# Five levels of a triangular inverse in one loop on quarters of the heads, with Y ahead of V behind it

## The chip, the cores and the metric

The kernel runs on one core of one Trainium2 chip. The metric is the device time of one execution, in microseconds; a kernel's time is the median over runs. A separate execution is profiled instruction by instruction, and its own time is given beside it.

## The reference

The program computes two transformer layers on one sequence of 256 tokens with 2048 features: a layer of two attention mixers, then a layer with an RWKV-7 recurrence beside a latent attention, and a gated feed-forward part. The change touches the recurrence alone. It has 16 heads of 64 features, and the reference runs it token by token:

```
def step(state, inp):
    r_t, w_t, k_t, v_t, a_t, b_t = inp
    sa = jnp.einsum('bhvk,bhk->bhv', state, a_t)
    state = (state * w_t[:, :, None, :]
             + sa[..., None] * b_t[:, :, None, :]
             + v_t[..., None] * k_t[:, :, None, :])
    return state, jnp.einsum('bhvk,bhk->bhv', state, r_t)
```

## The kernel before

Every engine has its own instruction stream, written out by hand, and semaphores join them. Most of the time goes to matrix products of a token block with weights that are split in a high and a low part (lines 973 to 1040 on TensorE, 1830 on ScalarE, 626 on GpSimd). Between the attention of the second layer and its output product stands the recurrence, called the scan here.

The scan cuts the 256 tokens into NCH = 4 chunks of 64. In a chunk it forms small 64x64 products for each of the 16 heads, inverts a unit lower triangular 64x64 matrix per head, and carries a 64x64 state to the next chunk. The heads stand in two sets `s` of 8: four pairs `q`, one head of a pair on partitions 0 to 63 and one on 64 to 127 (`halves`). A product for a set is 8 matmuls of 64x64, written by the generator `each`; each uses one quadrant of the array. With `swap=False` they use the two diagonal quadrants, with `swap=True` the other two; `in_turn` interleaves two generators, so that a swapped and an unswapped one run side by side. Every fp32 matmul shows as two records in the trace, so a product of a set is 16 records. Each set owns four PSUM banks (0 to 3).

The inverse is built by doubling in levels `m` = 1 to 5. In level m:

- GpSimd masks the matrix (`below_level`, M_m, line 900) into a buffer `LM`;
- TensorE makes T_m = M_m times X into bank 3 (`level_t`); VectorE adds the identity on its way out (`T2`, line 2695);
- TensorE makes X_m and Z_m from T_m side by side, into banks 0 and 1 (`level_xz`); ScalarE copies X_m out (line 2168), VectorE copies Z_m out (line 2705). In level 5 only Z_5, the inverse, is made.

The order on TensorE within chunk c: LB with P1 of chunk c-1; L; AK with U of chunk c-1; T1; S (the state's update) of chunk c-1; X1 and Z1; BK (transposed tokens, bank 2, copied by ScalarE at line 2189); then levels 2, 3 and 4 in an engine loop, `pe.Fori`, one pass a level, waits computed from the pass number (`wait_turn`); behind it, written out, level 5, Y of chunk c-1 (the outputs) and V, in this order: T5 in turn with the first half of Y, the second half of Y, V, Z5. After the last chunk P1, U and Y of chunk 3 follow. ScalarE copies P1, U, Y and V out (lines 2176 and 2168). ScalarE's last part has this order: P1 of chunk 3, four copies of the attention's output (line 2196), U, Y. TensorE then sums the outputs (line 1678) and starts the output product.

## Time and profile before

| | us |
|---|---|
| median of 3 runs | 1897.81 (1895.79 to 1908.44) |
| the profiled execution, its own time | 1894.01 |
| its span, first to last instruction | 1892.3 |
| the scan on TensorE, first LB to the sum behind the last Y | 943.58 to 1046.46 |

| engine | busy in the span | share |
|---|---|---|
| PE (TensorE) | 1832.4 us | 97% |
| POOL (GpSimd) | 1371.3 us | 72% |
| DVE (VectorE) | 1124.3 us | 59% |
| ACT (ScalarE) | 803.1 us | 42% |

Times in the views are microseconds from the span's start. PE rows are matmuls; a row's length counts the stay of the last matmul in the array. "issue" is time in which an engine waited for nothing that the profile shows. The chain of waits is followed back from the last instruction. The profiled execution is 3.8 us below the median.

### The profile page before, as it was taken

To read this page: it belongs to the slowest core of one execution; us is meant where nothing else is said; L and a number is where in the kernel's file an instruction comes from. 1 tells how busy PE (TensorE), PEld (TensorE's weight loads), DVE (VectorE), ACT (ScalarE), POOL (GpSimd) and SP (SyncE) were. 2 spreads that over 40 slices of the span, in tenths; PEclk is the share of its full clock that TensorE was granted. 3 is DMA by queue.
4 is the path that set the end of the run, shared out by engine and by line. 5 is a ranking of instruction groups with operands and counts; after the bars stand their busy time and mean duration, and the time that the engine had idled before them with its cause. 6 is when DMAs were issued, how large, how long until landed. Compare 5 with 4: busy or idle time off the path is not lost.

```text
span 1892.3 us, 31908 instructions
## 1 busy us (share of the span) xinstructions
PE 1832.4 (97%) x12663; PEld 1530.5 (81%) x12663; DVE 1124.3 (59%) x1207; ACT 803.1 (42%) x1079; POOL 1371.3 (72%) x693
## 2 busy tenths in 40 slices
PE   6999999999999999999898999999999999999998
PEld 3777778888668898888688788888888888788886
DVE  1225858560343546878664664788888888933235
ACT  4234444444454554343423554433333344343334
POOL 3657878888339889965353898999999989844443
PEclk9999999999999999999999999999999999999999
DMA  9996545555785565543200356655555555655552
GB/s 341 357 358 216 178 156 178 189 190 183 263 287 178 163 204 193 187 135 136 67 4 4 134 178 201 194 184 191 186 187 190 181 195 179 222 194 186 197 197 92
DMA packets 191066, 352.48 MB, mean 186 GB/s; under 512 B 6991, under 2 KB 52445, under 8 KB 188413
## 3 DMA queue, kind: packets, MB, share of 16 engines
q1 hardware_dynamic: 189580, 346.31, 55.5%
q10 hardware_dynamic: 1393, 4.83, 0.6%
q8 instruction: 70, 1.15, 0.2%
q14 instruction: 23, 0.19, 0.0%
HBM read 349.02 MB, written 2.10 MB: 186 GB/s over the span
## 4 chain that ended last, share of the span: by engine, by line
PE 66%; POOL 10%; issue 9%; DVE 9%; DMA 2%; SPq 2%; ACT 2%; POOLq 0%; DVEq 0%; ACTq 0%
POOL WL L626 10%; PE bank L1033 9%; PE bank L973 9%; PE bank L978 9%; PE bank L974 8%; PE bank L1040 5%; PE bank L1500 4%; PE bank L1784 4%; PE bank L1779 4%; PE bank L1777 4%; DMA arena<-in_w_ada 2%; SPq L689 2%; DVE arena L2437 2%; DVE CV L2778 1%; PE bank L419 1%
## 5 line engine op out<-in xcount | busy, mean ns | idle before, releaser
L626 POOL TENSOR_TENSOR WL<-WR,WH 128x1024 fp32r<-128x1024 f32 (+2 forms) x524 | 1269.0, 2447 | 379.9 <-ACT WH L1830 302.1
L1830 ACT ACTIVATE WH<-WR 128x1024 fp32r<-128x1024 f32 (+1 forms) x556 | 571.0, 1036 | 741.4 <-PE bank L1040 320.1
L1033 PE MATMUL bank<-HX,WH 128*128 128x512 f32 x1840 | 461.5, 392 | 0.0
L1033 PEld LDWEIGHTS bank<-HX,WH 128*128 128x128 f32 x1840 | 331.0, 189 | 59.0
L973 PE MATMUL bank<-WH,HX 128*128 128x512 f32 (+2 forms) x864 | 340.2, 394 | 2.7 <-ACT arena L1926 1.4
L974 PE MATMUL bank<-WH,HX 128*128 128x512 f32 (+2 forms) x864 | 331.0, 384 | 0.0
L1040 PEld LDWEIGHTS bank<-HX,WL 128*128 128x128 f32 x1840 | 250.4, 190 | 22.0 <-POOL WL L626 4.7
L1040 PE MATMUL bank<-HX,WL 128*128 128x256 f32 x1840 | 257.8, 283 | 1.1 <-POOL WL L626 0.6
L978 PE MATMUL bank<-WL,HX 128*128 128x512 f32 (+2 forms) x864 | 227.3, 385 | 1.9 <-POOL WL L626 1.4
L973 PEld LDWEIGHTS bank<-WH,HX 128*128 128x128 f32 x864 | 162.7, 188 | 43.7 <-issue 11.8
L978 PEld LDWEIGHTS bank<-WL,HX 128*128 128x128 f32 x864 | 159.3, 188 | 35.2 <-POOL WL L626 5.8
L974 PEld LDWEIGHTS bank<-WH,HX 128*128 128x128 f32 x864 | 162.8, 188 | 30.7 <-issue 2.2
L626 DVE TENSOR_TENSOR WL<-WR,WH 128x1024 fp32r<-128x1024 f32 x42 | 53.4, 1274 | 142.0 <-ACT WH L1830 142.0
L1777 PE MATMUL bank<-WH,AH 128*128 128x512 f32 x320 | 124.6, 389 | 0.0
L1779 PE MATMUL bank<-WH,AL 128*128 128x512 f32 x320 | 124.5, 389 | 0.0
L2778 DVE TENSOR_SCALAR CV<-RAWF,cols 128x256 f32<-128x256 f32 x44 | 102.0, 2378 | 2.0 <-DVE RAWF L2536 2.0
L2783 DVE SCALAR_TENSOR_TENSOR CV<-RAWF,cols,CV 128x256 f32<-128x256 f32 x44 | 100.0, 2331 | 1.6 <-DVE CV L2778 1.5
L2437 DVE TENSOR_SCALAR arena<-arena,small 128x128 f32<-128x128 f32 x64 | 69.6, 1156 | 31.1 <-ACT small L1838 31.1
L1784 PE MATMUL bank<-WL,AH 128*128 128x512 f32 x320 | 85.7, 390 | 2.0 <-DVE WL L626 2.0
L900 POOL TENSOR_TENSOR arena<-half,masks 128x256 f32<-128x256 f32 x40 | 29.0, 744 | 69.0 <-DVE half L2683 48.1
L1784 PEld LDWEIGHTS bank<-WL,AH 128*128 128x128 f32 x320 | 60.0, 188 | 14.7 <-DVE WL L626 2.4
L1777 PEld LDWEIGHTS bank<-WH,AH 128*128 128x128 f32 x320 | 60.1, 188 | 12.5
(347 smaller groups left out, 2088.0 us busy)
## 6 DMA issues: line engine op xcount, KB each, us to landing
WR<-in_w_in SPq DMA_DIRECT2D x80, 1024.0 KB, 5.0
WR<-in_ffn_w_gate SPq DMA_DIRECT2D x44, 1024.0 KB, 5.2
WR<-in_ffn_w_up SPq DMA_DIRECT2D x44, 1024.0 KB, 5.1
WR<-in_ffn_w_down SPq DMA_DIRECT2D x42, 1024.0 KB, 5.0
arena<-in_w_ada SPq DMA_DIRECT2D x64, 512.0 KB, 9.0
WR<-in_w_out SPq DMA_DIRECT2D x32, 1024.0 KB, 5.0
WR<-in_w_in SPq DMA_DIRECT2D x32, 512.0 KB, 8.9
WR<-in_w_ada SPq DMA_DIRECT2D x16, 1024.0 KB, 5.0
```

What stands on the lines that cost most here:

```text
L626: last = eng.tensor_tensor(lo[:, k, :], raw[:, k, :], hi[:, k, :], ALU.subtract)
L973: pe.matmul(out, hx[:, 0, kk, o], w, start=start, stop=False, skip_group_check=True)
L974: return pe.matmul(out, hx[:, 1, kk, o], w, start=False, stop=False, skip_group_check=True)
L978: return pe.matmul(out, hx[:, 0, kk, t * P:(t + 1) * P], w, start=False, stop=stop, skip_group_check=True)
L1033: last = pe.matmul(BANK[(first + f) % 8][:, :].rearrange("p (h n) -> p h n", h=2), wh[:, k, f * P:(f + 1) * P], hx[:, :, kk, :], start=kk ...
L1040: last = pe.matmul(BANK[(first + f) % 8][:, 0:L], wl[:, k, f * P:(f + 1) * P], hx[:, 0, kk, :], start=False, stop=kk == KT - 1, skip_group ...
L1777: pe.matmul(BANK[2 * c + t][:, :], AH[:, g % 2, k, o], wh[:, k, :], start=first and k == 0, stop=False, skip_group_check=True)
L1779: last = pe.matmul(BANK[2 * c + t][:, :], AL[:, g % 2, k, o], wh[:, k, :], start=False, stop=False, skip_group_check=True)
L1784: last = pe.matmul(BANK[2 * c + t][:, :], AH[:, g % 2, k, t * P:(t + 1) * P], wl[:, k, :], start=False, stop=final and k == PK - 1, skip_g ...
L1830: act.activation(half(WH, nth(n) % 2, *w), half(WR, n % NSLOT, *w), ACT.Copy).then_inc(hi_ready, 1)
L2437: last = dve.tensor_scalar(v, v, hr[:, g:g + 1], None, ALU.mult)
L2778: own.mark(dve.tensor_scalar(CV[:, f, :], RAWF[:, f, 2:L + 2], w(2), cols[:, ds(4 * i + (cb + f), 1)], ALU.mult, ALU.add))
```

## The change

The heads are treated in four quarters `g` (set `g // 2`, two of its four pairs) from level 2 on, and level 5 goes through the loop, which so makes four passes and not three.

- In a pass TensorE makes T for the four quarters, 4 matmuls each, then X and Z for the four, 8 matmuls each. Level 5 makes an X too, which nobody copies. Even quarters use bank 3 for T and Z and bank 0 for X, odd ones bank 1 for T and Z and bank 2 for X.
- VectorE copies T of all quarters and Z of quarters 0 and 1, ScalarE X of all quarters and Z of quarters 2 and 3, each copy 128x128 and not 128x256. T of a quarter now waits for the copy of its Z as well as of its X, since both use one bank.
- Bank 2 holds BK before the loop, so TensorE waits for both copies of BK ahead of it.
- The buffer for M5 is dropped: M2 to M5 share one, and each waits for T of the level before of both quarters of its set.
- Behind the loop stands Y of chunk c-1 alone, then V. Y and V wait for the copies of Z5; P1 of the next chunk still waits for the copy of V.
- In ScalarE's last part U is copied ahead of the four copies of the attention's output.

```diff
-        LM = [[at(18432 + 1280 * s_ + 256 * i, 4, N) for i in range(3)] for s_ in range(2)]
+        LM = [[at(18432 + 1280 * s_ + 256 * i, 4, N) for i in range(2)] for s_ in range(2)]
...
-                if m in (3, 4):
-                    P_.wait(pool, f"T{m - 1}_{s}", c)
-                elif c >= 1:
-                    P_.wait(pool, f"T{4 if m == 2 else m}_{s}", c - 1)
-                L_.mark(pool.tensor_tensor(LM[s][min(m - 1, 1) if m < 5 else 2], LBr[c % 2][s][:, :, 1, :],
+                if m == 1 and c >= 1:
+                    P_.wait(pool, f"T1_{s}", c - 1)
+                elif m >= 3 or (m == 2 and c >= 1):
+                    P_.wait(pool, f"T{m - 1 if m >= 3 else LEVELS - 1}_{2 * s + 1}", c if m >= 3 else c - 1)
+                L_.mark(pool.tensor_tensor(LM[s][min(m - 1, 1)], LBr[c % 2][s][:, :, 1, :],
                                            level[m].unsqueeze(1).to_broadcast([P, 4, N]), ALU.mult), f"M{m}_{s}")
...
+            def taken_z(g, c):
+
+                (D_, A_)[g // 2].wait(pe, f"Z{LEVELS - 1}_{g}", c)
...
                     AS_.wait(pe, f"P1_{s}", c)
-                    D_.wait(pe, f"Z{LEVELS - 1}_{s}", c)
+                    taken_z(2 * s, c)
+                    taken_z(2 * s + 1, c)
...
+                j, g = (0, s) if m == 1 else (1, s % 2)
+                set_, bank, qs = (s, 3, range(4)) if m == 1 else (s // 2, (3, 1)[g], range(2 * g, 2 * g + 2))
+                return four(set_, bank, 0, N, (of_pair(LM[set_][j]), of_pair(Xi[set_])), swap=m > 1, qs=qs)
...
+            def level_xz(g, c):
+
+                s, qs = g // 2, range(2 * (g % 2), 2 * (g % 2) + 2)
+                z, t2 = of_pair(Zi[c % 2][s]), of_pair(T2[s])
+                x_last, z_last = in_turn(each(s, (0, 2)[g % 2], 0, N, (z, t2), swap=True, qs=qs),
+                                         each(s, (3, 1)[g % 2], 0, N, (t2, z), qs=qs))
+                P_.mark(x_last, f"X2_{g}")
+                P_.mark(z_last, f"Z2_{g}")
...
-                with pe.Fori(0, LEVELS - 3) as i:
-                    for s in range(2):
-                        L_.wait_turn(pe, f"M2_{s}", c, i, 2)
-                        A_.wait_turn(pe, f"X1_{s}", c, i, 2)
+                for s in range(2):
+                    B_.wait(pe, f"BK_{s}", c)
+                with pe.Fori(0, LEVELS - 2) as i:
+                    for g in range(4):
+                        if g % 2 == 0:
+                            L_.wait_turn(pe, f"M2_{g // 2}", c, i, 2)
+                        (D_, A_)[g // 2].wait_turn(pe, f"Z1_{g}", c, i, 6)
+                        A_.wait_turn(pe, f"X1_{g}", c, i, 6)
                         pe.sem_inc(level_begun, 1)
-                        for last in level_t(2, s):
-                            pass
-                        P_.mark(last, f"T2_{s}")
-                    for s in range(2):
-                        D_.wait_turn(pe, f"T2_{s}", c, i, 4)
+                        P_.mark(level_t(2, g), f"T2_{g}")
+                    for g in range(4):
+                        D_.wait_turn(pe, f"T2_{g}", c, i, 6)
                         pe.sem_inc(level_begun, 1)
-                        level_xz(2, s, c)
-                P_.again(LEVELS - 4, 6)
-
-                for s in range(2):
-                    L_.wait(pe, f"M{LEVELS - 1}_{s}", c)
-                    A_.wait(pe, f"X{LEVELS - 2}_{s}", c)
-                    t = level_t(LEVELS - 1, s)
-                    if c == 0:
-                        for last in t:
-                            pass
-                    else:
-                        state_wait("Y", s, c - 1)
-                        last, _ = in_turn(t, state_part("Y", s, c - 1, range(2)))
-                    P_.mark(last, f"T{LEVELS - 1}_{s}")
+                        level_xz(g, c)
+                P_.again(LEVELS - 3, 12)
+
                 if c >= 1:
                     for s in range(2):
-                        for last in state_part("Y", s, c - 1, range(2, 4)):
+                        taken_z(2 * s + 1, c)
+                        state_wait("Y", s, c - 1)
+                        for last in state_part("Y", s, c - 1):
                             pass
                         S_.mark(last, f"Y_{s}")
                 for s in range(2):
+                    taken_z(2 * s + 1, c)
                     P_.mark(four(s, 0, 0, N, (of_set(v_, s), unit)), f"V_{s}")
-                for s in range(2):
-                    D_.wait(pe, f"T{LEVELS - 1}_{s}", c)
-                    level_xz(LEVELS - 1, s, c)
...
+            def take_quarter(name, m, g, c, dst):
+
+                s, h = g // 2, slice(2 * (g % 2), 2 * (g % 2) + 2)
+                bank = {"X": 0, "Z": 1}[name] if m == 1 else {"X": (0, 2), "Z": (3, 1)}[name][g % 2]
+                P_.wait(act, f"{name}{m}_{s if m == 1 else g}", c)
+                A_.mark(act.activation(dst[:, h, :], heads4(BANK[4 * s + bank][:, 0:4 * N])[:, h, :], ACT.Copy), f"{name}{m}_{g}")
...
-                for m in range(1, LEVELS - 1):
-                    for s in range(2):
-                        take(f"X{m}", s, c, 0, 0, flat4(Xi[s]))
+                for m in range(1, LEVELS):
+                    if m < LEVELS - 1:
+                        for g in range(4):
+                            take_quarter("X", m, g, c, Xi[g // 2])
+                    for g in (2, 3):
+                        take_quarter("Z", m, g, c, Zi[c % 2][1])
...
             take_state("P1", NCH - 1)
+            take_state("U", NCH - 1)
             for g in range(4):
                 act.activation(HH[:, 8 + 2 * g:10 + 2 * g, :], YMT[:, 2 * g:2 * g + 2, :], ACT.Copy).then_inc(y_hi, 1)
-            take_state("U", NCH - 1)
             take_state("Y", NCH - 1)
...
+                for m in range(2, LEVELS):
+                    for g in range(4):
+                        s, h = g // 2, slice(2 * (g % 2), 2 * (g % 2) + 2)
+                        P_.wait(dve, f"T{m}_{g}", c)
+                        D_.mark(dve.tensor_tensor(T2[s][:, h, :], bank4(s, (3, 1)[g % 2])[:, h, :],
+                                                  I2.unsqueeze(1).to_broadcast([P, 2, N]), ALU.add), f"T{m}_{g}")
+                    for g in range(2):
+                        h = slice(2 * g, 2 * g + 2)
+                        P_.wait(dve, f"Z{m}_{g}", c)
+                        D_.mark(dve.tensor_copy(Zi[par][0][:, h, :], bank4(0, (3, 1)[g])[:, h, :]), f"Z{m}_{g}")
```

On TensorE, the start of the loop's body before: T of set 0, T of set 1, then X and Z (32 matmuls in all) in two groups. Waits are named by the semaphore of the engine waited for (act_step is ScalarE's copies, dve_step VectorE's, pool_step GpSimd's masks).

```order
L1630 UNCONDITIONAL_BRANCH
L1630 ISA
L136 REGISTER_ALU [waits pool_step]
L1500 MATMUL bank<-arena 64x64 [waits act_step]
L1500 MATMUL bank<-arena 64x64 x7
L136 REGISTER_ALU
L136 REGISTER_ALU [waits pool_step]
L1500 MATMUL bank<-arena 64x64 [waits act_step]
L1500 MATMUL bank<-arena 64x64 x7
L136 ISA
L1500 MATMUL bank<-arena 64x64 [waits dve_step]
L1500 MATMUL bank<-arena 64x64 x15
```

The same place of the change: act_tokens ahead of the branch is the copy of BK.

```order
L1642 UNCONDITIONAL_BRANCH [waits act_tokens]
L1642 ISA
L136 ISA [waits pool_step]
L136 REGISTER_ALU [waits dve_step]
L1499 MATMUL bank<-arena 64x64 [waits act_step]
L1499 MATMUL bank<-arena 64x64 x3
L136 REGISTER_ALU
L136 REGISTER_ALU [waits dve_step]
L1499 MATMUL bank<-arena 64x64 [waits act_step]
L1499 MATMUL bank<-arena 64x64 x3
L136 REGISTER_ALU
L136 REGISTER_ALU [waits pool_step]
```

A wait stands ahead of every 4 matmuls of T, with register instructions ahead of each, where one stood ahead of every 8; 48 matmuls are in the body in both kernels.

On ScalarE, chunk 0 and the start of chunk 1 before (2 X1, 2 BK, then X2 to X4 and V, then P1 and U):

```order
L2168 ACTIVATE arena<-bank 128x256 [waits pe_step] x2
L2189 ACTIVATE half_64<-bank 128x512 [waits pe_step] x2
L2168 ACTIVATE arena<-bank 128x256 [waits pe_step] x8
L2176 ACTIVATE arena<-bank 128x256 [waits pe_state] x4
L2168 ACTIVATE arena<-bank 128x256 [waits pe_step] x2
```

and of the change:

```order
L2176 ACTIVATE arena<-bank 128x128 [waits pe_step] x6
L2200 ACTIVATE half_64<-bank 128x512 [waits pe_step] x2
L2176 ACTIVATE arena<-bank 128x128 [waits pe_step] x20
L2169 ACTIVATE arena<-bank 128x256 [waits pe_step] x2
L2184 ACTIVATE arena<-bank 128x256 [waits pe_state] x4
```

Six copies of 128x256 in three passes became 20 of 128x128 in four, and V's two copies stayed.

On TensorE behind the loop of chunk 1, before: the end of T5 in turn with Y (of which the last 17 matmuls are Y alone), V, and the two Z5:

```order
L1500 MATMUL bank<-arena 64x64
L1500 MATMUL bank<-half_64,arena 64x64 x17
L1500 MATMUL bank<-masks,arena 64x64 x16
L1500 MATMUL bank<-arena 64x64 [waits dve_step]
L1500 MATMUL bank<-arena 64x64 x7
L1500 MATMUL bank<-arena 64x64 [waits dve_step]
L1500 MATMUL bank<-arena 64x64 x7
```

and of the change, from the loop's end: Y of set 0 and set 1, V of both, then LB with P1 of the next chunk:

```order
L1642 COMPARE_AND_BRANCH
L1499 MATMUL bank<-half_64,arena 64x64 [waits act_tokens,dve_step]
L1499 MATMUL bank<-half_64,arena 64x64 x15
L1499 MATMUL bank<-half_64,arena 64x64 [waits act_tokens,act_step]
L1499 MATMUL bank<-half_64,arena 64x64 x15
L1499 MATMUL bank<-masks,arena 64x64 [waits dve_step]
L1499 MATMUL bank<-masks,arena 64x64 x7
L1499 MATMUL bank<-masks,arena 64x64 [waits act_step]
L1499 MATMUL bank<-masks,arena 64x64 x7
L1499 MATMUL bank<-RA,Bv 64x128 [waits act_state,dve_state,act_step]
```

No Z5 stands between V and the P1 that waits for V's copy. Between two loops the change writes out 208, 256 and 272 matmuls, where 240, 288 and 304 stood.

## Rows read from the trace of the kernel before

**Rows 1.** The page: an engine's busy time, share, instructions.
```profile
PE 1832.4 (97%) x12663; PEld 1530.5 (81%) x12663; DVE 1124.3 (59%) x1207; ACT 803.1 (42%) x1079; POOL 1371.3 (72%) x693
```

**Rows 2.** Stretches: window, length, busy us (records) of PE, PEld, DVE, ACT, POOL, clock.
```profile
943.50:963.10 19.60, 18.00 (x640) 17.10 (x642) 11.99 (x27) 5.06 (x13) 10.06 (x14) 1.00 0.07 27
...
985.50:1011.80 26.30, 22.88 (x905) 21.60 (x904) 14.24 (x33) 7.33 (x18) 10.04 (x14) 1.00 0.01 4
```

**Rows 3.** Chain of waits through chunk 2's loop: start, us, what.
```profile
1001.14 0.27 issue
1001.41 0.70 PE bank L1500 x16
...
1002.13 0.43 DVE arena L2695
1002.57 0.14 issue
1002.70 1.16 PE bank L1500 x64
...
1006.58 0.06 issue
1006.64 3.60 PE bank L1500 x144
```

**Rows 4.** Groups by shape in the scan: busy us, mean ns, idle before.
```profile
L1500 PE MATMUL bank<-arena 64*64 64x64 f32 x1984 | 56.7, 222 | 6.2 <-ACT arena L2168 1.9 <-issue 1.3 <-DVE arena L2695 0.9
L2695 DVE TENSOR_TENSOR arena<-bank,masks 128x256 f32<-128x256 f32 x40 | 16.5, 421 | 12.7 <-PE bank L1500 12.1
L2691 DVE TENSOR_TENSOR half<-bank,masks 128x512 f32<-128x512 f32 x8 | 5.2, 679 | 0.5 <-PE bank L1500 0.5
L2168 ACT ACTIVATE arena<-bank 128x256 f32<-128x256 f32 x40 | 15.3, 383 | 41.8 <-PE bank L1500 40.1
```

**Rows 5.** Timeline: copies that follow each other without a wait.
```profile
948.08 1.27 DVE L2691 TENSOR_TENSOR half<-bank,masks 128x512 f32<-128x512 f32 x2
949.27 0.74 DVE L2695 TENSOR_TENSOR arena<-bank,masks 128x256 f32<-128x256 f32 x2
...
1040.94 0.65 ACT L2176 ACTIVATE arena<-bank 128x256 f32<-128x256 f32 x2
```

**Rows 6.** Timeline of PE behind the last loop: V, then Z5.
```profile
1034.81 1.11 PE L1500 MATMUL bank<-masks,arena 64*64 64x64 f32 x32
1035.74 0.93 PE L1500 MATMUL bank<-arena 64*64 64x64 f32 x26
```

**Rows 7.** Timeline at chunk 0's loop entry: first T2 on PE, BK's second copy.
```profile
952.63 2.34 PE L1500 MATMUL bank<-arena 64*64 64x64 f32 x93
```
**Rows 8.** The same place on ACT.
```profile
952.89 0.60 ACT L2189 ACTIVATE half<-bank 128x512 f32<-128x512 f32 x1 [0.34 <-PE bank L1500]
```

**Rows 9.** PE's waits in the scan: us in total, times, longest.
```profile
PE bank L1500 <- issue: 3.5, 7, 1.1
PE bank L1500 <- ACT arena L2176: 1.7, 1, 1.7
```

**Rows 10.** DMA queues, the written-out stretch 982 to 998.7 us.
```profile
q8 instruction: 4, 0.07, 1.6%
```

**Rows 11.** DMA queues, inside chunk 2's loop, 1001.5 to 1007.5 us.
```profile
DMA packets 0, 0.00 MB, mean 0 GB/s; under 512 B 0, under 2 KB 0, under 8 KB 0
```

**Rows 12.** Chain of waits, the scan's end.
```profile
1038.97 2.07 ACT HX L2196 x4
...
1041.37 4.59 PE bank L1500 x96
```

**Rows 13.** Stretches of one us in the last Y (columns as in Rows 2).
```profile
1042.00:1043.00 1.00, 1.00 (x25) 1.00 (x22) 0.00 (x0) 0.00 (x0) 0.08 (x1) 0.50 0.06 16
```

**Rows 14.** Chain of waits behind the scan.
```profile
1046.46 3.67 PE bank L1678 x8
...
1067.34 21.94 POOL WL L626 x14
```

73 lines of the change are left out of this document (33 added, 40 removed).

## The prediction, made before the result was known

> **What bounds the kernel now.** The page comes first: TensorE is busy for 97% of the span, GpSimd for 72% [rows 1]. Such a share is a mean over stages, so the next view is the one by stretches, laid over the scan, the only place that the change touches. One chunk takes about 26 us there, with TensorE busy for 22.9 of 26.3 and VectorE for 14.2 [rows 2]. The whole scan is 102.9 us, 5.4% of the span, so a change of 1% of the kernel (19 us, about what a measurement of this kernel can tell from no change) would be a fifth of it. Then the chain of waits. In the scan it runs over TensorE and, in every pass of the loop, over one copy of VectorE [rows 3]. Behind the scan it goes straight on with the sums and, from 1067 us, with GpSimd's splitting [rows 14]. All of that starts from the last Y, so what the scan gains or loses goes into the time one to one.
>
> A pass before: 0.70 us for the first T (0.48 of array work and 0.22 that the last matmul stays), 0.02 and 0.43 for its copy, 0.14 to the first X and Z, 1.16 for both sets (0.94 and 0.22), 0.27 to the next T; together 2.72 us [rows 3, 4]. The array works for 1.88 of them (half a T takes 0.47, half of X and Z too), and this is what quarters can fill. At the loop's exit the same place has 0.06 in place of 0.27 [rows 3], so 0.21 is the price of going round.
>
> **The change, part by part: a pass.** The 4 quarters of T take 0.235 each, X and Z the same, 1.88 in all. Counted from the start of T: the first quarter has left the array at 0.235 + 0.22 and its copy starts at 0.48. A copy of 128x128 isn't in the trace. VectorE takes 0.42 for 256 columns and 0.68 for 512 [rows 4], so about 0.29 for 128. Two copies in a row start 0.32 apart (0.74 less 0.42), two of 512 columns 0.59 apart [rows 5], so quarters could follow each other every 0.19. The first copy is done at 0.77, and X and Z could start at 0.91; the array comes free at 0.94. The fourth quarter could start at 1.61, and its turn is 1.65. So the array doesn't wait in the middle. The next T needs X and now Z of its quarter: the first X leaves at 1.42, is copied by 1.69, and lets T start at 1.83, before the array is free (1.88). ScalarE has six copies a pass, X0 to X3, Z2, Z3. Its 128x256 copies take 0.38 [rows 4], start 0.27 apart at the closest [rows 5], and a quarter takes about 0.27, starting 0.16 to 0.27 after the one before. Z3 then starts at 2.45 to 2.67 and lets the fourth T go at 2.86 to 3.08. Its turn is 0.70 after the pass starts, so the pass can't be shorter than 2.16 to 2.38. With array, stay and turn-round it is 1.88 + 0.22 + 0.27 = 2.37.
>
> The loop's body also holds 24 instructions that aren't matmuls, where 12 stood (register sums and semaphore steps). No row has their price. From below it is nothing: before, those ahead of the second T are hidden. From above, the 0.21 of going round buys about six of them, 0.035 each, so 0.42 a pass for 12. I take 0.13, near the lower end, since most stand behind queued matmuls: a pass of 2.5 us, and 2.29 for the last (0.06 at its end). Before, a loop took 2.72 + 2.72 + 2.51 = 7.95; now 3 x 2.5 + 2.29 = 9.8, with level 5 in it. That is **+1.85 a chunk, +7.4**.
>
> The fixed part of a copy is what speaks against quarters. The Trainium skill (VectorE: DVE Perf Modes, the section on the TRN2 errata) gives a PSUM copy 120 cycles and its columns on VectorE, 172 on ScalarE, and says that many small tiles pay the fixed part each time. That would be 0.26 and 0.25 for a quarter, an estimate from that page, where the rows lead me to 0.29 and 0.27. Held for all of that, ScalarE's six copies would take 1.5 us a pass, and the fourth T would ask for a pass of 2.36. By the page alone the sum below would be 2 us less.
>
> GpSimd's masks wait for two quarters of T and share a buffer. At 0.74 each they would be done 1.45 and 2.2 into the pass, and are needed at 2.5 and 2.97. If that cover were gone, their excess would go into every pass.
>
> **Behind the loop.** Removed are the T5 and Z5 that were written out. Y of a late chunk is 96 records, 2.8 us at 16 in 0.47, and T5 and Y together took hardly more: the stretch from 1006.64 lasts 3.60 with most of V in it [rows 3]. T5 used the other two quadrants and was free there; in chunk 0 it wasn't (0.94). Z5 took 0.93 in each chunk [rows 6]. Together **-4.7**. But Z5 also hid the copy of V for which P1 waits. Now P1 comes 0.22 + 0.02 + 0.38 + 0.14 = 0.76 after V of set 0, of which V of set 1 hides 0.47: 0.29 each, **+1.2**.
>
> **Ahead of the loop.** The first T followed BK without a gap, at 952.63 [rows 7]. BK's second copy ends at 953.49 [rows 8], and 0.14 more is needed: +1.0, and 0.1 for the jump into the loop behind it. What queues behind this wait is the whole loop. **+4.4** over four chunks.
>
> **The end of the scan.** Four copies of the attention's output stand ahead of U on ScalarE, 2.07 us, and the last Y waits for U [rows 12]; this is TensorE's longest wait in the scan, 1.7 us [rows 9]. U of set 0 leaves the array as those copies begin, so Y would start some 1.75 earlier. Behind that gap the granted clock is 0.50, TensorE's lower level of 1.2 GHz, and 25 records a microsecond pass [rows 13] where 34 would. At full clock Y takes 2.8, and here it took 4.4: 1.55 more, which goes too if the idle time before it goes. **-3.3**. The output's four copies then lie under Y, and GpSimd needs them later.
>
> **Loading of the code.** TensorE has 3.5 us in the scan in which it waited for nothing shown [rows 9], all between loops, where 4 instruction packets of 16 KB come in 16.7 us [rows 10], and none inside a loop [rows 11]. The change writes out 32 fewer matmuls between two loops and has new waits under which loading goes on. That is worth 0 to -3.5; I take half, **-1.8**.
>
> Sum: 7.4 - 4.7 + 1.2 + 4.4 - 3.3 - 1.8 = +3.2. The profiled execution took 1894.0, so 1897.2; that execution was 3.8 below the median of the runs shown, so on their footing **1901**.
>
> **The rivals.**
> *Lighter passes.* The turn-round vanishes under more waiting matmuls (0.2 in 12 passes, -2.5), the control instructions cost nothing (-2.1) and all code stalls go (-1.7): 1895. For it: the second T of a pass starts without a gap now. Against: 0.27 stands at every turn of the loop. Chance 0.15.
> *Copies and control instructions become the limit.* Twelve small copies a pass for six larger ones (ScalarE six for two), each with its own wait. If ScalarE's quarters cost as much as today's 0.38, with arrivals in between, Z3 is done near 3.7 and the pass is 3.1: +0.6 x 16, 1911. Against: two copies in a row start 0.27 apart. Chance 0.15.
> *The quarters don't overlap as drawn*, and a pass stays at 2.72: +3.5, 1904; it lies inside my own range and has no chance of its own.
> *Slower: the loop has to load its code.* Its body grows from 60 to 72 instructions as written. None is loaded inside a loop now [rows 11]; outside, packets come one in 4.2 us [rows 10]. If the larger body made each of 16 passes wait for one packet, a pass would take 4.2 and the time be 1.7 x 16 = 27 more, 1928. It decides (over 1%) from a pass of 3.6. Against: the growth is small, and packets fell behind only in written-out code. Chance 0.05. The Trainium skill (Runtime: NRT & Kernel Launch, Instruction fetch mechanics) says that code comes in blocks of 256 instructions and that a taken branch to a block no longer held waits for a load. The trace agrees on the packets; a branch that waits for one is in no row.
>
> **How the numbers follow.** My forecast, 0.60: 1901, own range 1895 (pass 2.37, stalls gone) to 1907 (pass 2.8, stalls kept). Lighter passes 0.15, copies 0.15, code 0.05, and 0.05 for what I don't see. The range to hold 8 in 10 goes from 1893 to 1912. Faster by over 1% needs 19 us out of a scan of 103, which no mechanism here gives: 0.01. Slower by over 1% is the code rival and a little of the copies: 0.07. Within 1%: 0.92.
>
> **What would show it.** Right: four passes a chunk of about 2.5 us; TensorE idle about 1.1 us ahead of each loop until BK's copy; no granted clock of 0.5 in the last Y, which takes 2.8; idle time without a releaser well under 3.5; a scan of about 106 us. Wrong: passes of 3 us ended by ScalarE's Z copies; instruction packets inside a loop; a gap ahead of the last Y as before; the scan's length unchanged while the kernel's is not.

## The result, and the profile after

The changed kernel takes 1910.55 us in the median of 5 runs (1907.88 to 1913.44), against 1897.81 for the kernel before; the ratio is 1.0067 with an interval of 1.0035 to 1.0099. Timed once more, on another chip, it was 1.0084 (1.0067 to 1.0101). So it is slower by 0.7 to 0.8%, within 1%, some 13 to 16 us. The forecast was 3.2 us slower, 1901, with a range up to 1912: the side and the class were right and the time lies inside the range, but the slowdown is four times the forecast one.

The profiled execution takes 1911.6 us, its span is 1909.9. Most shares of the page have hardly moved from [rows 1], as 12.7 us in 1900 can't move them:

```profile
PE 1845.3 (97%) x12791; PEld 1542.6 (81%) x12791; DVE 1126.0 (59%) x1239; ACT 814.8 (43%) x1151; POOL 1370.7 (72%) x693
```

The chain of waits through chunk 1's loop is where one sees it (start, us, what), to be read beside [rows 3]:

```profile
980.34 0.60 ACT arena L2200
980.94 0.63 issue
981.58 2.74 PE bank L1499 x96
984.31 0.27 ACT arena L2176
...
984.68 2.69 PE bank L1499 x94
...
987.68 2.71 PE bank L1499 x94
...
990.70 2.63 PE bank L1499 x94
```

The four passes start at 981.58, 984.68, 987.68 and 990.70, and Y at 993.42: 3.10, 3.00, 3.02 and 2.72. The forecast was 2.5, 2.5, 2.5 and 2.29. Ahead of the first stand 0.60 for BK's copy, as foreseen, and then 0.63 in which TensorE waits for nothing shown, where 0.14 and 0.1 were put.

Inside a pass, stretches that begin at each quarter of T of chunk 0's second pass (window, length, busy us and records of PE, PEld, DVE, ACT, POOL, clock, DMA share, GB/s):

```profile
959.99:960.33 0.34, 0.34 (x9) 0.34 (x9) 0.00 (x0) 0.28 (x2) 0.00 (x0) 1.00 0.00 0
960.33:960.76 0.43, 0.43 (x13) 0.34 (x9) 0.28 (x1) 0.00 (x0) 0.00 (x0) 1.00 0.00 0
960.76:961.19 0.43, 0.43 (x10) 0.34 (x9) 0.30 (x2) 0.00 (x0) 0.33 (x1) 1.00 0.00 0
961.19:961.44 0.25, 0.25 (x11) 0.25 (x10) 0.20 (x1) 0.00 (x0) 0.25 (x1) 1.00 0.00 0
961.44:962.46 1.02, 1.02 (x70) 1.02 (x66) 0.87 (x4) 0.53 (x3) 0.87 (x2) 1.00 0.00 0
962.70:963.10 0.40, 0.00 (x0) 0.02 (x1) 0.00 (x0) 0.40 (x4) 0.00 (x0) 1.00 0.00 0
```

T's quarters follow each other after 0.34, 0.43 and 0.43 us, where 0.25 is what the fourth takes before X and Z begin (8 records in 0.23, and a gap of 0.02). A window counts PE as busy through such gaps, because a matmul's row is 0.22 long; by the starts of the matmuls the gaps are 0.106, 0.199 and 0.198. In the last line nothing stands on TensorE for 0.40 us. The chain puts that idle time down to ScalarE (L2176), since the copies in it are its own; but those are Z of quarters 2 and 3, and the T that comes next needs X and Z of quarter 0, whose copies ended at 962.21 and 962.27, 0.84 us before it starts at 963.11, and GpSimd's mask of its set, which ended at 961.59. So neither the copies nor the mask nor the array fill that time.

The rest of the scan, from the starts of the matmuls in both traces:

| stretch | before | after | difference | forecast |
|---|---|---|---|---|
| the four loops, first T to the first matmul behind | 32.4 | 47.9 | +15.5 | +7.4 |
| idle ahead of the four loops | 0.0 | 6.0 | +6.0 | +4.4 |
| from the last loop to the sum | 14.5 | 10.5 | -4.0 | -3.9 |
| all else between first LB and the sum | 56.0 | 51.2 | -4.8 | -4.7 |
| the scan | 102.9 | 115.6 | +12.7 | +3.2 |

The span is 17.6 longer: 12.7 in the scan, 2.7 ahead of it and 2.1 behind it, where the change touches nothing (the second profile below has 0.6 and 1.6 there). Of the 9.5 us by which the scan exceeds its forecast 8.1 are in the loops and 1.6 ahead of them.

The end came out as forecast. The chain of waits there, and a stretch of the last Y beside [rows 12, 13]:

```profile
1055.32 2.55 PE bank L1499 x80
...
1057.89 3.50 PE bank L1499 x112
...
1061.90 3.67 PE bank L1679 x8
```

```profile
1060.00:1061.00 1.00, 1.00 (x42) 1.00 (x39) 0.00 (x0) 1.00 (x4) 1.00 (x2) 1.00 0.00 0
```

Nothing waits for the output's copies, and the last Y runs at clock 1.00 with 42 records a microsecond; from its first matmul to its last it takes 2.80 us, where it took 4.35. TensorE's waits in the scan (us in total, times, longest), beside [rows 9]:

```profile
PE bank L1499 <- ACT arena L2176: 4.3, 11, 0.4
PE bank L1499 <- ACT arena L2200: 2.6, 2, 1.3
...
PE bank L1499 <- issue: 2.2, 5, 0.6
```

The 1.7 for U is gone. Issue fell from 3.5 to 2.2; in the second profile of the change it is 3.0. The new copies have the predicted sizes (busy us, mean ns):

```profile
L2176 ACT ACTIVATE arena<-bank 128x128 f32<-128x128 f32 x104 | 24.1, 278 | 49.8 <-PE bank L1499 49.3
L2726 DVE TENSOR_TENSOR arena<-bank,masks 128x128 f32<-128x128 f32 x64 | 18.6, 292 | 30.6 <-PE bank L1499 27.0
```

### The profile page after: what moved, and what is told of

The parts are those of the page before. It is cut to its first block, busy times and chain, and to the rows that moved or that the text cites. A ratio compares the mean times of both kernels' runs of the same rounds, so it can differ in the third digit from the quotient of the medians.

```text
span 1909.9 us, 32510 instructions
## 1 busy us (share of the span) xinstructions
PE 1845.3 (97%) x12791; PEld 1542.6 (81%) x12791; DVE 1126.0 (59%) x1239; ACT 814.8 (43%) x1151; POOL 1370.7 (72%) x693
## 4 chain that ended last, share of the span: by engine, by line
PE 74%; DVE 9%; POOL 5%; issue 5%; DMA 3%; SPq 2%; ACT 2%; DVEq 0%; POOLq 0%; ACTq 0%
PE bank L1032 15%; PE bank L972 8%; PE bank L977 8%; PE bank L973 8%; PE bank L1039 8%; PE bank L1499 5%; POOL WL L626 5%; PE bank L1785 4%; PE bank L1780 4%; PE bank L1778 4%; DMA arena<-in_w_ada 2%; SPq L688 2%; DVE arena L2448 2%; DVE CV L2799 1%; PE bank L1061 1%
## 5 line engine op out<-in xcount | busy, mean ns | idle before, releaser
L1499 PE MATMUL bank<-arena 64*64 64x64 f32 x2112 | 61.5, 229 | 10.4 <-ACT arena L2176 4.3
```

Of the source, the lines that this page charges most:

```text
L1499: yield pe.matmul(o[to, q, :], x(h, q), y(h, q), start=(n == 0), stop=(n == len(terms) - 1))
```

## Experiments

In the diffs, `-` and `+` are against the kernel that the text names. Ratios are against the kernel before on the same chip. "Scan" here is the time from the first matmul of LB to the last of Y: 102.1 in the kernel before, 114.9 and 115.7 in the two profiles of the change, so two executions of one kernel differ by up to 0.9.

### U ahead of the output's copies, alone (before_u_first)

```diff
             take_state("P1", NCH - 1)
+            take_state("U", NCH - 1)
             for g in range(4):
                 act.activation(HH[:, 8 + 2 * g:10 + 2 * g, :], YMT[:, 2 * g:2 * g + 2, :], ACT.Copy).then_inc(y_hi, 1)
-            take_state("U", NCH - 1)
             take_state("Y", NCH - 1)
```

> The kernel before with one part of the change alone: in ScalarE's last part U of chunk 3 is copied ahead of the four copies of the attention's output. Theory: those copies alone hold the last Y back, and the idle time they cause is also why the granted clock is 0.50 in it. Then no idle time of 1.7 us ahead of the last Y, no stretch at clock 0.50, a last Y of 2.8 us in place of 4.4, and a kernel 3.3 us faster (2.5 to 3.8). Rival: the idle time goes but the lower clock doesn't depend on it, and comes with something else that the tail does: 1.75 us faster. Rival: the output's copies are now late for GpSimd, which splits them right behind; then the gain goes and the time is within 1 us of before.

Measured: 0.9982 (0.9972 to 0.9992), 3.4 us faster. Second time, beside the last experiment:

> The kernel before with U of chunk 3 copied ahead of the attention's output, once more, beside mixed on one chip: 0.998 of the kernel before again (0.9972 to 0.9992), a scan of about 98.3 us to the last matmul. What mixed gains beyond this is the gain of quarters in the loop.

0.9988 (0.9979 to 0.9998). Scans of 98.3 and 99.2. In the chain of waits P1, U and Y run through, and the clock is 1.00 all along:

```profile
1033.05 7.06 PE bank L1500 x268
...
1040.12 3.51 PE bank L1500 x112
```

So this term (-3.3) stood, idle time and clock, and it is a gain without the rest of the change.

### The wait for BK inside the loop (bk_inside)

```diff
-                for s in range(2):
-                    B_.wait(pe, f"BK_{s}", c)
                 with pe.Fori(0, LEVELS - 2) as i:
...
                         pe.sem_inc(level_begun, 1)
+                        if g % 2:
+                            B_.wait(pe, f"BK_{g // 2}", c)
                         level_xz(g, c)
```

> The changed kernel with its wait for the copies of BK moved from ahead of the loop to where bank 2 is first overwritten: X of quarter 1 for set 0 and of quarter 3 for set 1, in the loop's body, as a wait for a constant on a matmul. In the change the first T of a loop starts 1.50 us behind the last BK matmul: BK's second copy ends 0.85 us behind it, and 0.64 is idle time without a releaser. Theory A: the wait for BK costs 0.85 and what follows it (the jump into the loop, its register instructions and waits), 0.64, was hidden before by queued matmuls and is hidden again: the first T follows within 0.1 to 0.2 us and the kernel is 4 x 1.3 to 4 x 1.4 = 5.2 to 5.6 us faster than the change. Theory B: the 0.64 is a cost of entering the larger loop, which no queue hides: then 0.64 stays, and the kernel is 4 x 0.85 = 3.4 us faster.

Measured: 1.0038 (1.0025 to 1.0050), 5.5 to 8.7 us below the change by its two ratios; the scan is 109.3, so 5.6 to 6.4 shorter. In the timeline BK's last 16 records start at 952.36 and the first T at 952.92, where in the change 1.50 lies between the last of BK's matmuls and T:

```profile
952.36 0.65 PE L1499 MATMUL bank<-masks,arena 64*64 64x64 f32 x16
952.92 1.21 PE L1499 MATMUL bank<-arena 64*64 64x64 f32 x24
```

The gap is 0.13. Theory A holds: the jump and the loop's first control instructions cost 0.64 behind a wait and 0.13 behind queued matmuls. The trace has them: behind the wait for BK come five (a move, three register instructions, one event with a wait), 0.09 to 0.11 us from one to the next.

### Two waits fewer in a pass (fewer_waits)

```diff
                         (D_, A_)[g // 2].wait_turn(pe, f"Z1_{g}", c, i, 6)
-                        A_.wait_turn(pe, f"X1_{g}", c, i, 6)
+                        if g < 2:
+                            A_.wait_turn(pe, f"X1_{g}", c, i, 6)
```

> The changed kernel without two of TensorE's waits in a pass of the loop: T of quarters 2 and 3 waits for ScalarE's copy of Z alone, which that engine makes behind its copy of X, so that the wait for X says nothing more. In the change T of quarters 1, 2 and 3 starts 0.106, 0.199 and 0.106 or 0.198 us behind the last matmul of the quarter before, although the copies they wait for had ended 0.3 to 0.7 us earlier; ahead of X and Z, with one wait, it is 0.020. Theory: each computed wait costs TensorE's sequencer about 0.09 us that four matmuls don't hide. Then the gap ahead of quarter 2 falls from 0.199 to about 0.106 and that ahead of quarter 3 from 0.106 to 0.198 down to 0.02 to 0.06, a pass gets 0.2 to 0.25 shorter and the kernel, 16 passes, 3 to 4 us faster than the change. Rival: the gap belongs to T's data (a copy that only seems done, or the bank that it overwrites); then the gaps stay and the time is that of the change.

The gap ahead of quarter 2 is mostly 0.106 in place of 0.199, that ahead of quarter 3 mostly 0.022 to 0.053. Passes in the chain of waits:

```profile
969.12 2.54 PE bank L1499 x94
...
971.98 2.57 PE bank L1499 x94
...
974.85 2.17 PE bank L1499 x76
```

969.12, 971.98, 974.85: 2.86 a pass. The gaps are where the theory has them, and the copies that T waits for are the same. The whole kernel has 1.0056 (1.0042 to 1.0071), 2 to 5 us below the change by its two ratios, which would fit the 3 to 4 of the theory, but its interval laps over the change's. The profiled scan of 115.3 is no shorter, because in this execution the clock was at 0.50 at the scan's start and for some three microseconds in two of the loops (more on that below). The mechanism is seen, its worth in time isn't settled by this run.

### TensorE's loop written out (written_out)

```diff
-                with pe.Fori(0, LEVELS - 2) as i:
+                for m in range(2, LEVELS):
                     for g in range(4):
                         if g % 2 == 0:
-                            L_.wait_turn(pe, f"M2_{g // 2}", c, i, 2)
+                            L_.wait(pe, f"M{m}_{g // 2}", c)
...
-                        pe.sem_inc(level_begun, 1)
...
```

> The changed kernel with the four passes of TensorE's loop written out: no registers, no jump, every wait a constant on the matmul itself; order and engines' work are the same. In the change a pass takes 3.0 to 3.2 us, of which T's four quarters 1.2 to 1.42 (0.94 of array work) and the turn 0.60 to 0.65. Theory: that excess is the control instructions. Written out, the gaps between quarters of T are 0.02 and the turn is 0.45 to 0.5 (stay, copy, start) wherever code is at hand, so a pass could take 2.4; but 48 matmuls more a pass must be loaded, and outside loops one packet of 16 KB of instructions (64 such matmuls) comes every 3.7 us or slower, which is 2.8 a pass. So passes of 2.8 to 3.0, the time that of the change or up to 4 us less, and idle time without a releaser in the passes. Rival (copies pace the pass): T's gaps stay at 0.1 to 0.2 and passes are 3.1 or, with the loading, longer: 5 to 15 us slower than the change.

Measured: 1.0047 (1.0031 to 1.0062), scan 110.2. Stretches that begin at the first T of chunk 0's passes 1, 2 and 3:

```profile
955.53:957.42 1.89, 1.88 (x96) 1.89 (x98) 1.40 (x6) 0.47 (x2) 1.12 (x2) 1.00 0.00 0
957.42:959.61 2.19, 2.19 (x108) 2.06 (x101) 1.61 (x7) 1.31 (x7) 1.57 (x3) 1.00 0.04 7
959.61:963.00 3.39, 2.64 (x117) 2.40 (x111) 1.69 (x7) 1.57 (x9) 1.59 (x3) 1.00 0.02 5
```

A pass takes 1.89, the array's own time, without any gap between T's quarters or at the turn; the next takes 2.19 (there T of quarter 2 starts 0.10 behind ScalarE's copy of its Z, so this is the limit that the copies set, put at 2.16 to 2.38 in the prediction). That is the same work on all engines as in the change, at 3.1 a pass. From the third pass on the code is late:

```profile
PE bank L1499 <- issue: 10.0, 14, 1.9
```

28 packets of instructions are loaded in the scan, 19 in the change. The theory held in kind; I had expected the loading to be felt from the first pass.

### One computed wait ahead of each T (joint)

```diff
                     for g in range(4):
-                        if g % 2 == 0:
-                            L_.wait_turn(pe, f"M2_{g // 2}", c, i, 2)
-                        (D_, A_)[g // 2].wait_turn(pe, f"Z1_{g}", c, i, 6)
-                        A_.wait_turn(pe, f"X1_{g}", c, i, 6)
+                        per = 2 + (g % 2 == 0)
+                        pe.wait_ge(t_ready[g], i * per + (c * per * (LEVELS - 2) + per))
                         pe.sem_inc(level_begun, 1)
...
```

> The changed kernel with one computed wait ahead of each T in place of two or three, from 14 to 8 in a pass: a semaphore of its own for each quarter, t_ready, is raised by the copy of X, by the copy of Z and (for quarters 0 and 2) by GpSimd's mask, and TensorE waits once for its count. Nothing else changes; every copy and matmul stays. In the loop with three, two and one such wait ahead of a T the gaps were 0.20, 0.106 and 0.02 us, the turn was 0.59 to 0.65 with three waits and, in the kernel before, 0.485 with two and 0.276 with none. Theory: 0.09 to 0.10 us of TensorE's sequencer for each computed wait, hidden only behind enough matmuls. Then gaps between quarters of 0.02 to 0.05, a turn of 0.38 to 0.45, a pass of 2.4 to 2.5 in place of 3.05, and a kernel 9 to 10.5 us faster than the change, about 1.0015 of the kernel before. Rival: with the waits out of the way the copies pace the pass (ScalarE makes six in it): gaps ended by ScalarE's Z copies, a pass of 2.6 to 2.8 and 4 to 7 us.

> The changed kernel once more, beside the others on one chip: 12 to 13 us slower than the kernel before (ratio 1.0067 again, 1.005 to 1.008), passes of 3.0 to 3.2, a first T 1.50 us behind the last BK matmul in all four chunks, a scan of 115 to 116 us. What lies outside the scan (2.7 us ahead of it and 2.1 behind it in the first profile of the change) should not come back, if it is a matter of the single execution.

The change itself: 1.0084 (1.0067 to 1.0101), scan 115.7. The 2.7 us ahead of the scan are 0.6 in this execution. Behind it 1.6 of the 2.1 are there again, but at another place: between 1663 and 1667 us, where the granted clock is 0.50 for 3.4 us, in lines that the change doesn't touch, and in some profiles of both families of kernels and not in others. So what lies outside the scan is a matter of the single execution.

joint: 1.0045 (1.0033 to 1.0058), 6.6 us below the change's median. Chunk 0's loop in the chain of waits:

```profile
955.87 2.23 PE bank L1504 x93
958.11 0.19 issue
958.29 2.25 PE bank L1504 x93
960.55 0.18 issue
960.73 2.22 PE bank L1504 x94
...
963.13 4.00 PE bank L1504 x139
```

Passes of 2.42, 2.44 and 2.40, gaps of 0.022 or 0.023 between T's quarters, a turn of 0.40 from matmul to matmul. ScalarE makes the same six copies, and is no limit; what the chain called ScalarE's wait in the change is 0.18 of issue here. The pass is the theory's, but the gain isn't all there: 6.6 of 10. Two of the four loops have a slow first pass. In chunk 1 it takes 4.21; in the timeline TensorE stops in the last X and Z of it:

```profile
979.23 2.15 PE L1504 MATMUL bank<-arena 64*64 64x64 f32 x91 [1.09 <-ACT arena L2207]
982.84 0.34 PE L1504 MATMUL bank<-arena 64*64 64x64 f32 x5 [1.46 <-issue]
```

The DMA queues of 980 to 982 us show what comes just before, one packet of instructions that starts at 980.55 (packets, MB, share):

```profile
q8 instruction: 1, 0.02, 2.9%
```

The Trainium skill (Runtime: NRT & Kernel Launch, Instruction fetch mechanics) has the next block fetched while the present one runs, the fetch mostly hidden; here, with the first pass at 2.4, it is not, and in the later passes nothing is loaded, as it was before [rows 11]. That the stop is a wait for this packet is read from its place in time: it ends 2.3 us behind the packet's start, and a stop of 1.3 us in the kernel before, one of 0.85 in written_out and one of 1.9 in joint_bk end 2.5 to 2.7 us behind theirs. No run takes the loading away. In chunk 3 of joint the first pass takes 4.58, a stop of that kind and the clock at 0.50 together.

### Both amendments (joint_bk)

> Both amendments together: one computed wait ahead of each T, and the wait for BK inside the loop at the first use of bank 2. If their gains are independent, as the theory has it (one lies in the passes, the other at the entry), this is 14.5 to 16 us faster than the change, and within 2 us of, or up to 0.25% faster than, the kernel before: passes of 2.4 to 2.5, entries of 0.05 to 0.15, a scan of about 100 us. Rival: both open the same slack, and instruction loading takes part of it back: a scan of 102 to 104, the idle time without a releaser up from 2.7 by 2 or more.

Measured: 1.0006 (0.9997 to 1.0015), 14 us below the change's median beside it, scan 103.3. So the 6 for the entries and 7 for the computed waits roughly add up, to 14.0 of the 14.4 us that the change had lost there, and the kernel with quarters and level 5 in the loop is level with the kernel before, though it has the gain at the end (3.4) in it. Passes are 2.4 to 2.5 but for some first ones, and no entry has a gap over 0.1. Part of the rival came true as well, stops for code: TensorE's waits in its scan have

```profile
PE bank L1504 <- issue: 7.7, 17, 1.7
```

of which the turns, 12 times 0.18, are 2.2.

### More waits in the kernel before (before_more_waits)

```diff
                         A_.wait_turn(pe, f"X1_{s}", c, i, 2)
+                        A_.wait_turn(pe, f"X1_{s}", c, i, 2)
+                        A_.wait_turn(pe, f"X1_{s}", c, i, 2)
                         pe.sem_inc(level_begun, 1)
```

> The kernel before with nothing but two more computed waits ahead of each T of the loop (the wait for X1 written three times; what it waits for is unchanged and long there). Theory, 0.09 to 0.10 us for each where nothing hides it: the turn grows from 0.485 to 0.67 to 0.69; ahead of the second T, where 8 matmuls stand in the queue, four waits need about 0.6 to 0.7 us against 0.47 of array work, so its gap grows from 0.02 to 0.15 to 0.25. A pass of 3.0 to 3.1 in place of 2.72, 12 passes, 3.5 to 4.8 us slower. Rival (a small price, 0.035 us for each of its two instructions, and only at the turn): pass 2.86, 1.7 us slower. Rival (computed waits are free where the semaphore has long stood): no change.

Measured: 1.0006 (0.9997 to 1.0015), 1.1 us slower by the medians, which the interval doesn't tell from nothing; the trace decides. The chain of waits through one turn, 0.27 before [rows 3]:

```profile
986.01 1.16 PE bank L1500 x64
987.17 0.38 issue
987.55 0.69 PE bank L1500 x16
```

The turn grew by 0.115 in most passes; ahead of the second T, with 8 matmuls queued, nothing is seen. My theory had 0.2 and 0.13 to 0.23 there. It falls by size, and the first rival (2.86 a pass) comes nearest to the 2.83 measured. The two added lines make one instruction more ahead of each T, an event, as both compare with a value that already stands in a register; one of the waits rides on the event that was there. So the unit of the price is not the wait that one writes. In the trace the next control instruction follows the added event after 0.111 us, which is what the turn grew by.

### One further control instruction of three kinds (price_probe)

```diff
                         per = 2 + (g % 2 == 0)
+                        if g == 1:
+                            pe.sem_inc(level_begun, 1)
+                        if g == 2:
+                            L_.wait(pe, "M1_0", c)
+                            pe.sem_inc(level_begun, 1)
+                        if g == 3:
+                            pe.wait_ge(t_ready[1], i * 2 + (c * 2 * (LEVELS - 2) + 2))
+                            pe.sem_inc(level_begun, 1)
```

> One look at joint_bk's loop with one control instruction more ahead of three of its quarters of T, a different one for each. In joint_bk the quarters 1, 2 and 3 each start 0.023 us behind the last matmul of the one before. Ahead of quarter 1 now stands an event more that waits for nothing; ahead of quarter 2 one that waits for a constant, long reached; ahead of quarter 3 one that waits for a computed value, long reached too, with its register sum. Theory (the price is that of each further instruction that waits for a computed value): 0.02 to 0.03, 0.02 to 0.03 and about 0.106, the gap that two computed waits had in the change. Rival (every control instruction costs its share, 0.035 to 0.05, once the matmuls no longer cover it): 0.06 to 0.08 ahead of quarters 1 and 2 and about 0.11 ahead of 3. Rival (waits cost, whatever they wait for): quarter 2 at 0.1 too.

Stretches from quarter to quarter in a steady pass (in joint_bk each is 0.25):

```profile
957.95:958.34 0.39, 0.39 (x8) 0.33 (x9) 0.00 (x0) 0.39 (x3) 0.00 (x0) 1.00 0.00 0
958.34:958.64 0.30, 0.30 (x10) 0.30 (x9) 0.20 (x1) 0.03 (x1) 0.00 (x0) 1.00 0.00 0
958.64:958.95 0.31, 0.31 (x14) 0.31 (x10) 0.20 (x2) 0.00 (x0) 0.07 (x1) 1.00 0.00 0
```

Gaps of 0.167, 0.072 and 0.071, from 0.023. An event that waits for a constant and one that waits for a computed value open the same 0.05 (the register of the latter was there already, so no sum was added). My theory, that it is the computed value, fell. The event that waits for nothing opens 0.14 ahead of quarter 1, but it is not dearer. The trace records the control instructions too (`PEldq` is TensorE's sequencer, the part that reads its instructions). These are the four events that the loop had, 51 ns long each:

```profile
L1657 PEldq EVENT_SEMAPHORE  x4: 51/51/51, 957.8 to 958.8; - x4
```

From the start of an event to the start of the next control instruction 0.151 us pass in all three stretches, whatever it waits for and whether or not four matmuls stand behind it, and 0.095 from the one register instruction, which stands ahead of quarter 1. So the sequencer needs 0.151 + 0.151 + 0.095 = 0.397 for quarter 1 and 0.302 for each of the others, and these are the stretches, 0.397, 0.302 and 0.301 from first matmul to first. Without the added events it needs 0.246 and 0.151, and four matmuls with the gap behind them take 0.25: both are hidden. The added event costs 0.151 everywhere; what differs is the slack, 0.007 ahead of quarter 1 and 0.10 ahead of the other two. The second rival is right in kind (each control instruction has its price once the matmuls ahead don't cover it), with a price of three to four times its 0.035 to 0.05 for an event.

### V ahead of Y (v_first)

```diff
-                if c >= 1:
-                    for s in range(2):
-                        taken_z(2 * s + 1, c)
-                        state_wait("Y", s, c - 1)
...
                 for s in range(2):
                     taken_z(2 * s + 1, c)
                     P_.mark(four(s, 0, 0, N, (of_set(v_, s), unit)), f"V_{s}")
+                if c >= 1:
+                    for s in range(2):
+                        taken_z(2 * s + 1, c)
+                        state_wait("Y", s, c - 1)
...
```

> One look at the changed kernel with V ahead of Y behind the loop, on TensorE and in ScalarE's copies. In the change P1 of set 0 starts 0.225 us behind V (it waits for V's copy; the prediction had 0.29), once in each of four chunks. Theory: with Y of 1.9 us between them that wait goes in chunks 1 to 3 and the scan is 0.6 to 0.9 us shorter, everything else the same. Rival: V, which overwrites what the loop's last X left and waits for a copy of Z5, now waits where Y filled the time: the gap behind the loop grows from 0.31 by as much, no change.

(ScalarE's copies of V and Y change places in the same way.) One execution: P1's wait of 0.225 in chunks 1 to 3 is 0.04, and the first matmul behind chunk 1's loop comes after 0.20, not 0.31, so the rival's growing gap isn't there. From the last X and Z of a loop to the last matmul of P1 the three boundaries are 0.22, 0.28 and 0.66 us shorter than in the change, whose two profiles agree on them within 0.01. The theory holds there, with 1.2 for its 0.6 to 0.9. The whole scan doesn't show it: 115.3 lies between the change's two, which differ by 0.9.

### Three passes in quarters, level 5 on sets (mixed)

```diff
-                with pe.Fori(0, LEVELS - 2) as i:
+                with pe.Fori(0, LEVELS - 3) as i:
...
+                for s in range(2):
+                    L_.wait(pe, f"M{LEVELS - 1}_{s}", c)
+                    if s == 0:
+                        A_.wait(pe, f"X{LEVELS - 2}_1", c)
+                    (D_, A_)[s].wait(pe, f"Z{LEVELS - 2}_{2 * s + 1}", c)
+                    t = each(s, 3, 0, N, (of_pair(LM[s][2]), of_pair(Xi[s])), swap=True)
...
```

(against joint_bk; T5, Y, V and Z5 then stand as in the kernel before)

> A version that should beat both: joint_bk's loop, but with three passes (levels 2 to 4), and level 5 written out behind it on whole sets as in the kernel before (T5 in turn with the first half of Y, then the rest of Y, V, Z5), U ahead of the output's copies. Three passes at 2.42, the last without its turn, 7.0, against 7.95 in the kernel before with its larger waits; entry 0.05 to 0.15. Theory: against the kernel before 4 x 0.9 less in the loops, 3.4 less at the scan's end, and 0.5 more at the entries: 6.5 faster, ratio 0.9965, scan about 96 us to the last matmul (before 102.1). Rival: idle time that is gone here returns as waits for code between the loops (the written-out stretches are as long as before): only 3.5 to 4.5 faster, ratio 0.998, as with U's copy alone, and idle time without a releaser of 6 us and more.

Measured: 0.9982 (0.9970 to 0.9994), median 1890.52, beside 1892.63 for U's copy alone on the same chip. The scan is 96.3, 2.0 and 2.9 shorter than that kernel's two. Chunk 2's loop in the chain of waits:

```profile
999.59 2.67 PE bank L1508 x104
1002.26 0.18 issue
1002.44 2.21 PE bank L1508 x94
...
1004.84 1.99 PE bank L1508 x78
```

It beats the kernel before, by 3.4 of the 6.5 that the theory asked for, and so the change too. The rival's time is right; of its 6 us and more of idle time without a releaser there are 5.3: TensorE's issue is 5.3 in place of 3.5, and its turns, eight times 0.18, explain 1.4 of that; the rest is in the written-out stretches and first passes, up to 0.9 at once.

```profile
PE bank L1508 <- issue: 5.3, 16, 0.9
```

What quarters are worth over U's copy alone is 2.1 us by the medians and 1.1 by the ratios, which the two intervals don't tell apart; only the scans do.

## Why the prediction was right and wrong

*A pass of 2.5.* Wrong, it is 3.0 to 3.1, and this is most of the whole miss. The step that failed is the price of the control instructions: "0.035 each, so 0.42 a pass for 12. I take 0.13, near the lower end, since most stand behind queued matmuls". In a pass of 3.12 the array and its small gaps take 1.97 (1.88 put), T's three gaps 0.50 (nothing put), and the turn 0.65 (0.49 and a share of 0.13 put). The 12 instructions stand mostly ahead of T, and ahead of them are 4 matmuls, 0.23 us, which don't cover two or three waits, as the kernel before's 8 do. Joint, with six computed waits fewer, has the gaps at 0.02 and a pass of 2.42; written_out, with none, has 1.89 and 2.19. Even my upper bound gave 2.79. It was made by dividing 0.21 by six.

What the runs show in its place is in the records of the control instructions. In the change's loops the next one follows a register instruction after 0.09 to 0.11 us, an event ahead of T after 0.151, one ahead of X and Z after 0.171, the taken branch after 0.266 (medians; matmuls behind an event are in these times). Summed over the 24 that is 2.97 a pass, where the passes take 3.00 to 3.12. So TensorE's sequencer set the whole pass and the array waited for it: T's quarters are 0.34 and 0.43 apart, as two or three register instructions and an event need. "No row has their price" held for the rows chosen, not for the trace: the kernel before has the same steps at its turn (0.097, 0.27, 0.108, 0.097 and 0.107 us). The Trainium skill (Advanced Engine Details and Errata, Network/Comms) has 50 to 100 ns for a sequencer's reading of a semaphore; the event's record of 51 ns agrees, but the 0.11 to 0.17 us until the next instruction lie above it.

*What the turn is made of.* "Array, stay and turn-round, 1.88 + 0.22 + 0.27". By the number nearly right for the loop, by the reason wrong: I took the turn for the time that data need, and put a queue's price on top. Written out, the turn is 0.02, because quarter 0's copies ended long before. All of 0.6 is control (0.94 from the last event of X and Z over the branch to the first T, less the 0.35 that the last matmuls cover), and it grows with the waits ahead of the first T: 0.40 with one, 0.485 with two (before), 0.60 with three. The prediction had the numbers to see it, 0.06 at the exit against 0.27 at the turn, and used them as a price of going round only.

*The copies.* Right: 0.28 and 0.29 for a quarter (0.27 and 0.29 put), the limit that they set 2.19 (2.16 to 2.38 put). The rival "copies and control instructions become the limit" got its time right (3.1, 1911) for half of a reason: its sum is ScalarE's copies at 0.38, and these play no part. It had 0.15, and its other half was the cause.

*Ahead of the loop.* 1.50 for each entry, not 1.1. BK's copy is there as put; behind it come 0.64, not 0.24. Bk_inside gives 5.6 to 6.4 of the scan back. The step that failed was "0.14 more is needed, and 0.1 for the jump": five control instructions stand between the wait and the first matmul, and a wait exposes them all at once.

*The end of the scan.* Right: -3.3 put, -3.4 and -2.3 measured alone, with the clock at 1.00 once the idle time is gone.

*Behind the loop, and code.* -4.7, +1.2 and -1.8 were put; with the share of the last chunk set apart, -4.7 was put for the first three boundaries and -4.8 found. The term for code, half of 3.5, isn't settled: issue fell by 1.3 in one profile of the change and by 0.5 in the other. P1 waits 0.225, not 0.29.

*The loop loads its code.* Not in the change: no packet of the queue that loads TensorE's code (q8) comes in passes 2 to 4 of chunk 1. But joint has stops for code in first passes, up to 1.7 us at a time, once passes are light; with the clock at 0.50 in chunk 3 they make two of its loops 1.7 and 2.1 us longer than the other two, which is most of what is missing from its 10 us. That the change's slow passes covered such stops is a guess.

*What would show it.* Of the five signs named, those on the end and, in one profile of two, on issue came true; entries (1.5 for 1.1) and scan (115 for 106) did not, and that on passes named its own failure ("passes of 3 us ended by ScalarE's Z copies"), which the page indeed prints and which is misleading: ScalarE is named because its copy ended last before T, not because T needs it.

## What to carry to other kernels

Cutting a step of an engine loop into quarters multiplies the waits of the engine that issues, and each must be hidden by the matmuls that stand ahead of it: count the control instructions for each group of matmuls, at about 0.09 us for a register instruction and 0.15 for an event, and compare the sum with the group's own time (0.25 us for four of these matmuls, 0.49 for eight). The longer of the two is what the group takes. Before splitting, merge: one semaphore per quarter that all its producers raise turned 14 computed waits into 8, and a pass of 3.05 into 2.42. Where a wait stands ahead of a loop, put it at the first instruction inside that needs it; and where the profile names a releaser, look up when the operand really needed was ready.

## What the runs showed of the hardware

Behind idle time of 1.3 to 1.9 us TensorE's clock can fall. In the first profile of the change, stretches at the start of chunk 2's loop, behind 1.5 us of idle time:

```profile
1011.00:1012.00 1.00, 1.00 (x35) 1.00 (x35) 0.42 (x2) 0.00 (x0) 0.47 (x2) 0.50 0.06 16
1012.00:1013.00 1.00, 1.00 (x50) 1.00 (x46) 0.69 (x3) 0.55 (x2) 0.64 (x1) 0.50 0.00 0
```

0.50 is the lower level, 1.2 GHz. The other three entries of that execution, with the same idle time, kept 1.00; in the second profile and in v_first it was chunk 2's again, in fewer_waits chunks 2 and 3, in joint chunk 3. With the wait moved inside and nothing else (bk_inside) no stretch of the scan is at 0.50. But it needs no entry: in joint_bk, whose entries have no idle time, the clock is 0.50 from 982.2 to 985.6, behind a stop of 1.9 us that ended at 980.3. The loop concerned takes 12.41 in place of 11.85. Why one entry is hit and the next not is open.

The other surprise is how completely control instructions hide as long as they fit: one register instruction and a wait ahead of joint's quarter 1 need 0.246 us beside matmuls of 0.25, and its gap is 0.023; in before_more_waits those ahead of the second T need 0.47 beside 0.49, and the added wait isn't seen at all. One event more on the first of these opened 0.144.
